# Attention values with V as the stationary operand, one key-value group per half of the array's columns, and a new order of the work in a step

## The reference

```
# branch b: sliding window, sinks; branch a: top-k selected keys; 8 heads, 2 key-value heads, head size 64
logits = einsum('bqgrd,bqkgd->bqgrk', q, k) * 64**-0.5      # masked
p = softmax(logits)                                         # branch b with one more sink logit
o = einsum('bqgrk,bqkgd->bqgrd', p, v)
y_a = o_a @ w_branch_a ;  y_b = o_b @ w_branch_b
x = x + (sigmoid(g_a) * y_a + sigmoid(g_b) * y_b) @ w_out
```

## Time and profile before

| | us |
|---|---|
| median of 3 runs | 1600.77 |
| lowest, highest | 1600.43, 1602.52 |
| profiled execution, its own time | 1602.53 |
| its span in the trace | 1600.7 |
| TensorE busy | 1586.0 (99%) |
| VectorE busy | 764.5 (48%) |
| GpSimd busy | 708.6 (44%) |
| ScalarE busy | 503.7 (31%) |

### The profile page before, as it was taken

How to read it: one execution, slowest core, us unless ns; L and a number is a source line. 1 busy time by engine, 2 the same in 40 slices (tenths; PEclk the granted TensorE clock), 3 DMA queues, 4 the chain that set the end, 5 groups by cost and what they waited for, 6 DMA issues and landing times.

```text
span 1600.7 us, 19536 instructions
## 1 busy us (share of the span) xinstructions
PE 1586.0 (99%) x7590; PEld 1312.8 (82%) x7590; DVE 764.5 (48%) x1098; ACT 503.7 (31%) x745; POOL 708.6 (44%) x273
## 2 busy tenths in 40 slices
PE   9999999999999999999999999999999999999998
PEld 6887788888888988888888887877778988888886
DVE  6701588910166566666005389976563431023203
ACT  3012211210125444344124344247533442124312
POOL 5875189677761354454452003321133244344451
PEclk9999999999999999999999999999999999999999
DMA  5242032232333333333323222310034122323221
GB/s 205 98 132 79 1 111 80 82 128 80 105 106 105 93 93 105 95 89 105 105 81 112 81 80 79 106 53 27 28 106 132 49 84 106 105 79 106 105 95 63
DMA packets 123285, 147.00 MB, mean 92 GB/s; under 512 B 5143, under 2 KB 98375, under 8 KB 123208
## 3 DMA queue, kind: packets, MB, share of 16 engines
q1 hardware_dynamic: 121334, 141.05, 27.3%
q10 hardware_dynamic: 1874, 4.85, 0.9%
HBM read 143.79 MB, written 2.10 MB: 91 GB/s over the span
## 4 chain that ended last, share of the span: by engine, by line
PE 95%; POOL 2%; issue 1%; DVE 1%; ACT 1%; DMA 0%; SPq 0%; DVEq 0%; POOLq 0%; ACTq 0%
PE ps L631 28%; PE ps L632 28%; PE ps L633 28%; PE ps L773 3%; PE ps L850 2%; PE ps L1029 2%; PE ps L1015 1%; POOL w_lo L584 1%; PE ps L838 1%; POOL w_hi L579 1%; PE ps L909 1%; PE ps L871 0%; DMA raw<-in_w_up 0%; POOL spare_lo_out L584 0%; PE ps L811 0%
## 5 line engine op out<-in xcount | busy, mean ns | idle before, releaser
L584 POOL TENSOR_TENSOR w_lo<-raw,w_hi 128x1024 fp32r<-128x1024 f32 x224 | 557.0, 2507 | 721.7 <-ACT w_hi L1073 719.0
L631 PE MATMUL ps<-hT_hi,w_hi 128*128 128x512 f32 (+1 forms) x928 | 356.6, 384 | 0.8 <-POOL w_lo L584 0.5
L632 PE MATMUL ps<-hT_lo,w_hi 128*128 128x512 f32 (+1 forms) x928 | 355.3, 383 | 0.0
L633 PE MATMUL ps<-hT_hi,w_lo 128*128 128x512 f32 (+1 forms) x928 | 355.2, 383 | 0.0
L1073 ACT ACTIVATE w_hi<-raw 128x2048 fp32r<-128x2048 f32 (+1 forms) x87 | 165.0, 1896 | 245.6 <-PE ps L631 211.1
L631 PEld LDWEIGHTS ps<-hT_hi,w_hi 128*128 128x128 f32 x928 | 174.8, 188 | 37.0 <-issue 2.3
L633 PEld LDWEIGHTS ps<-hT_hi,w_lo 128*128 128x128 f32 x928 | 174.8, 188 | 33.7
L632 PEld LDWEIGHTS ps<-hT_lo,w_hi 128*128 128x128 f32 x928 | 174.9, 188 | 33.4
L579 POOL TENSOR_TENSOR w_hi<-raw,cells 128x2048 fp32r<-128x2048 f32 x35 | 130.1, 3716 | 129.2 <-PE ps L631 127.6
L633 PE MATMUL ps<-w_hi,f_lo 128*128 128x512 f32 x400 | 155.8, 390 | 0.0
L631 PE MATMUL ps<-w_hi,f_hi 128*128 128x512 f32 x400 | 155.8, 390 | 0.0
(11 more groups left out here) (303 smaller groups left out, 2212.0 us busy)
## 6 DMA issues: line engine op xcount, KB each, us to landing
raw<-in_w_in SPq DMA_DIRECT2D x86, 512.0 KB, 4.6
raw<-in_w_up SPq DMA_DIRECT2D x76, 512.0 KB, 4.6
raw<-in_w_down SPq DMA_DIRECT2D x54, 512.0 KB, 4.1
raw<-in_w_out SPq DMA_DIRECT2D x16, 512.0 KB, 4.1
raw<-in_w_ret_o SPq DMA_DIRECT2D x8, 512.0 KB, 4.1
raw<-in_w_sgu_o SPq DMA_DIRECT2D x8, 512.0 KB, 4.2
x<-in_x SPq DMA_DIRECT2D x4, 512.0 KB, 6.0
raw<-in_w_branch_b SPq DMA_DIRECT2D x4, 512.0 KB, 4.2
```

The source lines that it names most:

```text
L584: nc.gpsimd.tensor_tensor(lo[:, c], raw[:, s, c], hi[:, c].bitcast(f32), ALU.subtract).then_inc(unit_split, 1)
L631: first = nc.tensor.matmul(dst, a_hi, b_hi, start=start, stop=False)
L632: nc.tensor.matmul(dst, a_hi, b_lo, start=False, stop=False)
L633: return first, nc.tensor.matmul(dst, a_lo, b_hi, start=False, stop=stop)
```

## The change

The values matmul is turned round. V (128 x 64) is stationary, `probs_T` (128 x 128) moves. Group 0 writes partitions 0 to 63 and group 1 partitions 64 to 127 of the same columns, so each group sits in one half of the array's columns. The result comes out transposed, and the old transposes of `o2` go. In their place the reciprocals (tokens on partitions) are spread to 512 columns by VectorE (`wide_ri`), transposed by TensorE (`out_T`), copied to SBUF by ScalarE (`ri_T`), and multiplied with the values' bank by VectorE into `oTb`, for both branches. For branch a ScalarE then rounds `oTb` to `oTa_hi` and VectorE makes `oTa_lo` from two SBUF tiles, a step later (`o_split`).

The order within a step becomes: logits of pair p, values of pair p-4, transposes of pair p-2, out_T, a_T, parts. The reciprocals (`sums`) come at p % 4 == 1, the product stays with out_T at p % 4 == 3. There is one step more, and the last three parts stand in steps 34, 35, 36 instead of 34, 34, 35. Heads now lie on partitions in another order, so the rows of w_branch_a and w_branch_b are loaded in two halves of 64 partitions (`load_heads`). Values matmuls, transposes and dense matmuls keep their numbers; VectorE has 8 instructions more and ScalarE 5.

```diff
--- before.py
+++ after.py
@@ -41,7 +41,7 @@
 HEAD = [0, 4, 1, 5, 2, 6, 3, 7]
 GA_IN = 7
 GA_PARTS = 4 * (KT - GA_IN)
-PARTS = [2 + 4 * n for n in range(GA_PARTS)] + [23 + n * 11 // 13 for n in range(13)] + [34, 34, 35]
+PARTS = [2 + 4 * n for n in range(GA_PARTS)] + [23 + n * 11 // 13 for n in range(13)] + [34, 35, 36]
 A_T_AT = [2, 3, 4, 5, 6]
 
 
@@ -59,13 +59,17 @@
 
 
     steps = []
-    for p in range(PAIRS // 2 + 4):
+    for p in range(PAIRS // 2 + 5):
         step = []
-        for kind, back in (("logits", 0), ("probs_T", 2), ("values", 3)):
+        for kind, back in (("logits", 0), ("values", 4), ("probs_T", 2)):
             if 0 <= p - back < PAIRS // 2:
                 step += [(kind, 2 * (p - back)), (kind, 2 * (p - back) + 1)]
+        if p > 4 and p % 4 == 1:
+            step.append(("sums", p // 4 - 1))
         if p > 4 and p % 4 == 3:
             step.append(("out_T", p // 4 - 1))
+        if p > 4 * NT + 4 and p % 4 == 0:
+            step.append(("o_split", p // 4 - 2))
         step += [("a_T", n) for n, at in enumerate(A_T_AT) if at == p]
         step += [("part", n) for n, at in enumerate(PARTS) if at == p]
         steps.append(step)
@@ -80,12 +84,12 @@
 def has_ticket(kind, n):
     if kind == "part":
         return part_of(n)[2] == part_of(n)[3] - 1
-    return kind != "values"
+    return kind not in ("values", "sums", "o_split")
 
 
 ATTENTION = attention_steps()
 EVENTS = [e for step in ATTENTION for e in step]
-ACT_EVENTS = in_order(lambda e: 0 if e[0] == "probs_T" else 1)
+ACT_EVENTS = in_order(lambda e: 0 if e[0] in ("probs_T", "o_split") else 1)
 DVE_EVENTS = in_order(lambda e: {"logits": 2 * (e[1] % 2), "probs_T": 1}.get(e[0], 3))
 TICKETED = [e for e in EVENTS if has_ticket(*e)]
 RETENTION = [("scores", 0), ("scores", 1), ("values", 0), ("scores", 2), ("values", 1),
@@ -336,7 +340,8 @@
         above = at("above", [P, S], B2 + 40 * KB)
         equal = at("equal", [P, S], B2 + 42 * KB)
         upto = at("upto", [P, S], B2 + 44 * KB)
-        o2 = at("o2", [P, 2, S], B2 + 48 * KB)
+        wide_ri = at("wide_ri", [P, 2, S], B2 + 48 * KB)
+        ri_T = at("ri_T", [P, S], B2 + 52 * KB)
         ik2 = at("ik2", [P, NT, 2, HD], B2 + 50 * KB)
         ik_gain = at("ik_gain", [P, 2, HD], B2 + 52 * KB)
         ik_stat = at("ik_stat", [P, 64], B2 + int(52.5 * KB))
...
@@ -463,6 +470,14 @@
                     parts = [(dst[:, h:h + k // 2, :], src[:, h:h + k // 2, :]) for h in (0, k // 2)]
                 for h, (part, of) in enumerate(parts):
                     sp.dma_start(part, of).then_inc(raw_loaded[u % 2] if u or per else first_loaded[h], 16)
+
+            def load_heads(u, src):
+
+                sp.wait_ge(unit_split, 2 * (u - 1))
+                dst = raw[:, u % 2, :].rearrange("p (k n) -> p k n", k=4)
+                for g in range(KV_HEADS):
+                    of = src[g * 4 * HD:(g + 1) * 4 * HD, :].rearrange("(k p) n -> p k n", p=HD)
+                    sp.dma_start(dst[g * HD:(g + 1) * HD, :, :], of).then_inc(raw_loaded[u % 2], 16)
 
             def load_x(t):
                 sp.dma_start(x[:, t, :], a["x"][0, t * P:(t + 1) * P, :]).then_inc(x_loaded[t], 16)
@@ -545,7 +560,7 @@
-                    load(U0[phase] + j, rows(name)[:, :, j * 512:j * 512 + 512], 4)
+                    load_heads(U0[phase] + j, a[name][:, j * 512:j * 512 + 512])

@@ -997,8 +1012,10 @@
                     continue
                 if kind == "out_T":
                     t = event("out_T", s)
-                    pe.wait_ge(o2_made, s + 1)
-                    transposes(t, [o2[:, s % 2, n * P:(n + 1) * P] for n in range(4)])
+                    pe.wait_ge(ri_made, s + 1)
+                    transposes(t, [wide_ri[:, s % 2, n * P:(n + 1) * P] for n in range(4)])
+                    continue
+                if kind in ("sums", "o_split"):
                     continue
                 turn, h = s // HEADS, HEAD[s % HEADS]
                 branch, tt = turn // NT, TILE[turn]
@@ -1017,20 +1034,24 @@
                 elif kind == "probs_T":
                     pe.wait_ge(probs_made, s + 1)
                     transposes(event("probs_T", s), [probs[:, s % 4, n * P:(n + 1) * P] for n in range(nk)])
-                else:
+                elif s % 2 == 0:
                     value = dsa_value if branch else swa_value
                     b = VALUES_BANK + turn % 2
                     if s % HEADS == 0 and turn < 2:
                         await_evacuated(pe, max(t for t in range(T0["attention"]) if BANK[t] == b))
                     elif s % HEADS == 0:
-                        pe.wait_ge(o2_made, turn - 1)
-                    await_evacuated(pe, event("probs_T", s))
+                        pe.wait_ge(o_made, turn - 1)
+                    for g in range(KV_HEADS):
+                        await_evacuated(pe, event("probs_T", s + g))
+                    col = slice(h % 4 * P, (h % 4 + 1) * P)
                     for n in range(nk):
-                        last = nc.tensor.matmul(ps[:, b, h * HD:(h + 1) * HD], probs_T[:, s % 4, n * P:(n + 1) * P],
-                                                value(k0 + n, h // 4), start=n == 0, stop=n == nk - 1)
-                    last.then_inc(values_made, 1)
-            for turn in range(NT, 2 * NT):
-                await_evacuated(pe, event("out_T", turn))
+                        for g in range(KV_HEADS):
+                            last = nc.tensor.matmul(ps[g * HD:(g + 1) * HD, b, col], value(k0 + n, g),
+                                                    probs_T[:, (s + g) % 4, n * P:(n + 1) * P],
+                                                    start=n == 0, stop=n == nk - 1)
+                            if n == nk - 1:
+                                last.then_inc(values_made[g], 1)
+            pe.wait_ge(oTa_made, NT)
             for j in range(2):
                 unit_T(U0["y_a"] + j, T0["y_a"] + 4 * j, 4, 512, oTa_hi, oTa_lo)
             long("out2", 4, m2_hi, m2_lo, ready=lambda k: pe.wait_ge(lo_made, 2 * KT + NT + k + 1), after="h4")
@@ -1337,7 +1358,7 @@
                     turn, h = s // HEADS, HEAD[s % HEADS]
                     nk = TILE[turn] + 1 if turn >= NT else min(TILE[turn] + 1, 2)
                     if s % HEADS == 0 and turn >= 2:
-                        act.wait_ge(o2_made, turn - 1)
+                        act.wait_ge(ri_made, turn - 1)
                     await_evacuated(act, event("logits", s))
                     nc.scalar.activation(probs[:, s % 4, 0:nk * P], probs[:, s % 4, 0:nk * P], ACT.Exp,
                                          bias=nm[:, turn % 2, h:h + 1], scale=-1.0,
@@ -1348,7 +1369,7 @@
                                              ACT.Exp).then_inc(sinks_exp, 1)
                     k = s - OTB_AT
                     if k == 0:
-                        await_evacuated(act, event("out_T", NT - 1))
+                        act.wait_ge(o_made, NT)
                     if 0 <= k < NT:
                         hi_out.up(nc.scalar.activation(oTb_hi[:, k, :], oTb[:, k, :], ACT.Copy))
                 elif kind == "probs_T" and s % 2:
@@ -1356,17 +1377,17 @@
                     nk = TILE[turn] + 1 if turn >= NT else min(TILE[turn] + 1, 2)
                     t = event("probs_T", s)
                     if s >= 4:
-                        act.wait_ge(values_made, s - 3)
+                        act.wait_ge(values_made[1], s // 2 - 1)
                     evacuate(t, probs_T[:, s % 4, 0:nk * P], ACT.Copy, ps[:, BANK[t], 0:nk * P])
                 elif kind == "out_T":
                     t = event("out_T", s)
-                    view = bank(t).rearrange("p (k n) -> p k n", k=4)
+                    if s:
+                        act.wait_ge(o_made, s)
+                    evacuate(t, ri_T[:, :], ACT.Copy)
+                elif kind == "o_split":
                     tok = slice(TILE[s] * P, (TILE[s] + 1) * P)
-                    if s < NT:
-                        evacuate(t, oTb[:, :, tok], ACT.Copy, view)
-                    else:
-                        await_psum(act, t)
-                        hi_out.up(nc.scalar.activation(oTa_hi[:, :, tok], view, ACT.Copy))
+                    act.wait_ge(o_made, s + 1)
+                    hi_out.up(nc.scalar.activation(oTa_hi[:, :, tok], oTb[:, :, tok], ACT.Copy))
                 elif kind == "a_T":
                     t = event("a_T", s)
                     if s < NT:
@@ -1868,31 +1889,36 @@
                     nk = TILE[turn] + 1 if turn >= NT else min(TILE[turn] + 1, 2)
                     t = event("probs_T", s)
                     if s >= 4:
-                        dve.wait_ge(values_made, s - 3)
+                        dve.wait_ge(values_made[0], s // 2 - 1)
                     await_psum(dve, t)
                     V.tensor_copy(probs_T[:, s % 4, 0:nk * P], ps[:, BANK[t], 0:nk * P]).then_inc(evacuated[BANK[t]], 1)
-                elif kind == "values" and s % HEADS == HEADS - 1:
```

(36 more changed lines are left out.)

6 lines of the change are left out of this document (4 added, 2 removed).

## The result

| | before | after |
|---|---|---|
| median, us | 1600.84 (8 runs) | 1605.88 (8 runs) |
| lowest, highest | 1599.54, 1603.15 | 1604.38, 1607.37 |
| profiled execution, its span | 1602.53, 1600.7 | 1606.61, 1604.8 |

The medians differ by 5.0 us; the ratio is given as 1.0026, with a 95% interval of 1.0016 to 1.0035. The change makes the kernel slower, by little, but clear of the noise. The forecast was 1601.3, which is 4.6 us too low: 1605.88 lies in the wide range of 1592 to 1609, but above the forecast's own one of 1598.5 to 1605. Some executions of most kernels here have a mean clock of about 0.91 over 1066 to 1085 us and others 1.00, which moves a time by about 2 us (both profiled executions here are of the first kind).

A forecast was written before the change was run, and what follows sets the result against it. TensorE's execution and waits were taken as the bound; terms 0.5 + 1.5 + 1.1 + 1.0 - 0.5 - 2.2 - 0.9 made +0.5 us, so 1601.3 us. Own range 1598.5 to 1605; 8 in 10: 1592 to 1609.

The forecast's parts named there:

- V after = 0.16 + 0.21k: Values matmul on overlapping column halves: 0.37, 0.58, 0.79, 1.00 us for one to four blocks, giving back about 9 us.
- rival B: Values matmuls: column halves run one after the other, 14.5 us more, 1616 us, or some 1609; chance 0.13.
- The old V: Values matmul before the change: about 0.45k - 0.09 us before dense work or transposes, 0.45k + 0.03 before logits.
- The wait that takes its place: Second logits matmul waits for VectorE's reduction, 1.01 us after transposes start; two-block step 2.23 us, 0.17 more than before.
- Rival A: Logits: the wait for VectorE's reduction does not bind, so the gains come whole, 1591 us; chance 0.16.
- Steps 3 to 6 and 12 to 23: Attention steps outside the first turn's end: waits against shorter values matmuls, +0.5 and +1.0 us in the two stretches.
- steps 16 to 19: Steps with logits of four blocks: 2.86 against 2.48 us twice, 3.08 against 2.92, 4.30 against 4.26; +1.0 us.
- Steps 7 and 8, +1.5: GpSimd's split slows VectorE's 8-column sum, delaying ScalarE's copy, the multiplication and step 9's logits by 1.16 us; +1.5 us.
- rival C: Attention phase: the granted clock falls in the new gaps; one fall 1603 us, three 1606; chance 0.21.
- The end, -0.9: Last dense parts: TensorE's waits of 1.21 and 0.73 us shrink to 0.2 and 0.3; -1.4, with 0.5 given back.
- Sum: All terms of the attention phase together: +0.5 us, own ends -2.5 and +4, giving 1601.3 us.
- Weights in halves, nothing: Loads of w_branch in halves of 64 partitions: same bytes and rows, nothing or below 0.1 us either way.

The follow-up runs named there:

- e3: Kernel before, old whole-array values, in the changed kernel's order (values before transposes), output transposes one step later: 1615.97 us, 1.0092 of before.
- e8: Changed kernel with six probability buffers instead of four, multiplication by ri_T one step later, GpSimd's y_b and y_a splits delayed: 1593.88 us, 0.9953 of before.
- e10: Changed kernel, its four probability buffers kept, with multiplication by ri_T one step later and GpSimd's y_b and y_a splits delayed: 1598.94 us, 0.999 of before.
- e5: Changed kernel with GpSimd's split of y_b's first unit waiting until after the sums of step 9: 1600.64 us, 0.9999 of before.
- e6: Changed kernel with VectorE's multiplication by ri_T one step later, in steps 8, 12, 16 and 20, behind both reductions: 1601.6 us, 1.0001 of before.
- e9: Changed kernel with GpSimd's split of y_a's first unit waiting for the third oTa_lo (step 32): 1604.41 us, 1.0021 of before.
- e7: Column-half values in the old step order, four probability buffers, multiplication by ri_T one step later, GpSimd's y_b and y_a splits delayed: 1594.14 us, 0.9954 of before.

## Why the prediction was right or wrong

*V after = 0.16 + 0.21k.* Right: V to T is 0.37, 0.58 to 0.59, 0.80 and 1.02 us for one to four blocks. The halves overlap; rival B is out. Its 9 us in all are 10.1 by e3, of which some 1.7 are e3's longer spell at the low clock. The old V was sized too low for this order: before transposes, two blocks take 0.95 us in e3 and not 0.81.

*The wait that takes its place.* Right, in place (second logits matmul, released by VectorE's reduction), in cause (e8 against e10) and in size where VectorE is free (2.24 against 2.23 us, e10). In the changed kernel itself, with the multiplication in the way, steps 12 and 13 took 2.54 and 2.43 us, against 2.37 and 2.23 forecast. Rival A is out for four buffers, and is what happens with six.

*Steps 3 to 6 and 12 to 23.* +0.67 and +1.43 against +0.5 and +1.0: near. Inside the second stretch larger errors offset each other, which is luck: steps 16 to 19 came at +0.4 instead of +1.0, step 23 at +0.55 instead of -0.26, step 15 at -0.2 instead of +0.5. Part of that is bookkeeping, since a step's wait stands inside the logits of the next one.

*Steps 7 and 8, +1.5.* The chain was right: the addition beside the split, ScalarE, the multiplication, a reduction; 1.34 us of idle time against 1.16 to 1.5. The step that failed is the next one: the sum left the clock out and put it into rival C, with 0.21, as if it were another case. Rival C is what came, and it was a consequence of this term: the prediction itself had 1.5 us of idle in step 9, and the earlier trace rows had shown TensorE busy 0.38 of 1.40 us with a clock of 0.58 behind it. Its price was too low as well, 1.6 us where e5 leaves 2.8: after this gap the clock was 0.50 over all of five microseconds. And the argument against it, single gaps of 0.4 us that cost nothing, was about gaps a third of this one. One fall was priced at 1603; the run had one fall, and of the 2.9 us from there 1.2 are its low price and most of the rest is the tail. The fall wasn't certain either: the 1.53 us gap in the tail left the clock at 1.00, and so did the gap at the start of the phase in e6 and e9 (TensorE busy 0.39 and 0.37 of 1.40 us, the clock 1.00 over the next four), where before, after, e7 and e8 have 0.57 or 0.58. What decides between them is not shown.

*The end, -0.9.* Too good by 1.8 us: steps 24 to 30 came as forecast (-2.2 against -2.1), so the miss of the last stretch is the end's. The wait at the dense part did not shrink but grew from 0.78 to 1.53 us, since the oTa_lo of step 32 took 2.07 us and the gate stood behind it. The prediction named this meeting, with the right duration beside it (1.89), and then gave back 0.5 us for all of it. e9 measures 1.33. The remaining 0.5 is open; the sum had taken 1.21 and 0.73 us from the rows of the weight loads, where the matmuls were idle for only 0.78 and 0.33, and so gave back more than there was. What was missing was to ask what TensorE waits for behind it on VectorE.

*Sum.* +5.05 us from step 3 to y_a, against +0.5; of the 4.55 between them 2.8 are the clock, 1.3 the tail's collision, and the rest terms of up to 0.7 us in both directions. The 1605.88 lies in the range of 8 in 10 because that range was made wide for the rivals, and not because the sum was right.

*Weights in halves, nothing.* Not tried by itself; the stretches leave no room for more than some tenths.

## What to carry to other kernels

Before a matmul is put last in a step, ask what its readers hold back: here a ring of four buffers made TensorE's next logits wait for the transposes, and two more buffers were worth 5.1 of the 9 us aimed at. If a forecast lets TensorE be idle as long as in a place of the profile that has a slow clock behind it, the slow clock belongs in the sum, times its chance, and not only among the rivals. And small VectorE instructions beside a long GpSimd one on SBUF are to be costed at the long one's pace, with all that is queued behind them; here a wait that let the GpSimd one run elsewhere cost nothing.
